# Six gather slots instead of eight, and one weight block kept in the freed room, in a two-layer decoder trunk

## What is computed

```
for l in range(DEPTH):                      # 2 layers
    x = x + mixer_l(rmsnorm(x))             # even: GLA + stick-breaking; odd: MoBA + RG-LRU
    x = x + memory_cross_attention(rmsnorm(x), rmsnorm(mem), ...)
    x = x + peer_ffn(rmsnorm(x), wq, subkeys, u, v)

def block(xi):                              # peer_ffn, for 128 tokens
    q = (xi @ wq).reshape(Tb, PEER_HEADS, 2, PEER_DQ // 2)
    s = jnp.einsum('thcd,hcnd->thcn', q, subkeys)
    ...                                     # top 16 of 128 x 128 key pairs for each of 8 heads
    ue = u[eidx]                            # eidx: 128 tokens x 8 heads x 16 experts
    ve = v[eidx]
    act = jax.nn.gelu(jnp.einsum('td,thkd->thk', xi, ue), approximate=False)
    return jnp.einsum('thk,thkd->td', (g * act), ve)
```

## Time and profile before

| | |
|---|---|
| median of 3 runs | 1721.77 us (1721.43 to 1725.01) |
| the profiled execution | 1724.17 us, its span 1722.4 us |
| PE busy | 1354.3 us, 79% of the span |
| DVE busy | 991.8 us, 58% |
| ACT busy | 717.6 us, 42% |
| POOL busy | 608.0 us, 35% |
| moved by DMA | 670.05 MB, 389 GB/s over the span |

### The profile page before, as it was taken

How to read it: one execution, slowest core, us unless ns; L and a number is a source line. 1 busy time by engine, 2 the same in 40 slices (tenths; PEclk the granted TensorE clock), 3 DMA queues, 4 the chain that set the end, 5 groups by cost and what they waited for, 6 DMA issues and landing times.

```text
span 1722.4 us, 24057 instructions
## 1 busy us (share of the span) xinstructions
PE 1354.3 (79%) x8582; PEld 702.3 (41%) x8582; DVE 991.8 (58%) x2464; ACT 717.6 (42%) x1990; POOL 608.0 (35%) x516
## 2 busy tenths in 40 slices
PE   8797999896798859787787669787788566766766
PEld 7676855553374216344354115344464111111111
DVE  1421498754567856654556876664548964445443
ACT  2322246544533434563533444563534443333332
POOL 0000122343333343233333453232334456655552
PEclk9898999898898979988889669998898676567566
DMA  9513799999999999999999999999999999999996
GB/s 385 202 49 123 303 424 421 379 407 422 422 421 423 420 423 423 421 422 422 421 421 422 421 407 424 421 421 422 422 421 404 422 421 421 421 421 421 421 421 255
DMA packets 86904, 670.05 MB, mean 389 GB/s; under 512 B 9584, under 2 KB 12032, under 8 KB 13568
## 3 DMA queue, kind: packets, MB, share of 16 engines
q0 software_dynamic: 73728, 536.90, 75.2%
q1 hardware_dynamic: 13056, 131.61, 18.6%
HBM read 667.43 MB, written 1.05 MB: 388 GB/s over the span
## 4 chain that ended last, share of the span: by engine, by line
DMA 41%; PE 38%; DVE 10%; ACT 5%; issue 4%; POOL 2%; SPq 0%; POOLq 0%; ACTq 0%; DVEq 0%; PEldq 0%
DMA arena<-in_experts,idxT 40%; PE psum L579 37%; DVE arena L1637 5%; POOL arena L2056 2%; ACT cst L1066 1%; ACT ring L1066 1%; DVE red L1606 1%; DVE cst L1598 1%; ACT gains L1066 1%; ACT L1066 1%; DMA ring<-in_ev_sq 0%; ACT gelus L1066 0%; DVE cst L1604 0%; PE psum L963 0%; ACT L1071 0%
## 5 line engine op out<-in xcount | busy, mean ns | idle before, releaser
L2056 POOL DMA_INDIRECT arena<-in_experts,idxT x512 | 607.8, 1187 | 1086.2 <-PE psum L579 831.2
L579 PE MATMUL psum<-arena,cst 64*64 64x512 f32 (+1 forms) x4102 | 687.7, 758 | 284.9 <-ACT cst L1066 283.8
L1637 DVE CUSTOM_DVE_ANT_0 arena<-arena,xrow 128x1024 f32<-128x1024 f32 x512 | 622.8, 1224 | 501.5 <-DMA arena<-in_experts,idxT 500.4
L1066 ACT ACTIVATE gelus<-red 128x1 f32<-128x1 f32 x512 | 103.4, 202 | 742.5 <-DVE red L1637 741.5
L579 PEld LDWEIGHTS psum<-arena,cst 64*64 64x64 f32 (+1 forms) x4102 | 130.3, 154 | 678.4 <-ACT cst L1066 599.5
L579 PEld LDWEIGHTS psum<-hT,ring 128*128 128x128 f32 x2368 | 285.0, 198 | 116.6 <-issue 110.7
L579 PE MATMUL psum<-hT,ring 128*128 128x128 f32 x2368 | 306.7, 287 | 25.1 <-DVE hT L1481 21.5
L1066 ACT ACTIVATE cst<-cst,gains 128x128 f32<-128x128 f32 x512 | 206.3, 403 | 16.8
L1066 ACT ACTIVATE gains<-gelus,gateT 128x1 f32<-128x1 f32 x512 | 150.8, 294 | 18.5 <-DVE gateT L1615 1.5
L579 PEld LDWEIGHTS psum<-mixT,ring 128*128 128x128 f32 (+1 forms) x592 | 70.1, 193 | 27.9 <-issue 25.4
L579 PE MATMUL psum<-mixT,ring 128*128 128x128 f32 (+1 forms) x592 | 76.9, 283 | 3.7 <-issue 3.0
(11 more groups left out here) (225 smaller groups left out, 844.9 us busy)
## 6 DMA issues: line engine op xcount, KB each, us to landing
ring<-in_pq SPq DMA_DIRECT2D x16, 2048.0 KB, 11.6
ring<-in_ev_out SPq DMA_DIRECT2D x4, 2048.0 KB, 9.6
ring<-in_xq SPq DMA_DIRECT2D x4, 2048.0 KB, 11.5
ring<-in_xo SPq DMA_DIRECT2D x4, 2048.0 KB, 11.5
arena<-in_experts,idxT POOLq DMA_INDIRECT x512, 15.3
ring<-in_od_out SPq DMA_DIRECT2D x4, 2048.0 KB, 12.0
ring<-in_ev_sq SPq DMA_DIRECT2D x2, 2048.0 KB, 10.2
ring<-in_ev_sk SPq DMA_DIRECT2D x2, 2048.0 KB, 12.2
```

The costliest lines, as they stand in the source:

```text
L579: return nc.tensor.matmul(out, lhsT, rhs, start=start, stop=stop)
L1066: return nc.scalar.activation(out, in_, f, **k)
L1637: V.tensor_tensor_reduce(out=ut, in0=ut, in1=xrow[:, u // PAIRS, :], scale=1.0, scalar=0.0, op0=ALU.mult, op1=ALU.add, accum_out=dots[:, k ...
L2056: nc.gpsimd.indirect_dma_start(slot[slot_of(u)], None, d["experts"], bass.IndirectOffsetOnAxis(ap=idxT[:, u:u + 1], axis=0))\
```

## The change

The slots of expert rows become six. The room of the other two (columns 12288 to 16383 of `arena`) becomes a fifth place for weights, number 4. `HELD` names one block for each layer that goes there: `ev_sq` and `od_rx`. Each is loaded once, for the front of the first half, and kept until the front of the second half has read it; `ev_sq1` and `od_rx1` vanish from the list. The other blocks alternate between the ring's slots as before, but counted without the held ones. Since 256 is no multiple of 6, the slot of a unit now counts through both layers.

```
+HELD = {"ev_sq": 4, "od_rx": 4}
...
-SLOTS = 8
+SLOTS = 6
...
     for t in range(TT):
         for n in ("sq", "sk", "sv", "qk", "gv", "gr"):
-            out.append((f"ev_{n}{t}", d[f"ev_{n}"], f"{n}.{t}"))
+            if t == 0 or f"ev_{n}" not in HELD:
+                out.append((f"ev_{n}{t}", d[f"ev_{n}"], f"{n}.{1 if f'ev_{n}' in HELD else t}"))
...
-    for b in range(len(blocks)):
-        s = b % RING if b < early else b % 2 if b < late else (b - late) % LATER_RING
+    turn = 0
+    for b, name in enumerate(names):
+        turn = 0 if b in (early, late) else turn
+        if name[:-1] in HELD:
+            s = HELD[name[:-1]]
+        else:
+            s = b % RING if b < early else turn % 2 if b < late else turn % LATER_RING
+            turn += 1
...
+        places = [ring[:, s, :] for s in range(RING)] + [arena[:, 3 * BLOCK:4 * BLOCK]]
...
-        def slot_of(u):
-            return (u + 1) % SLOTS
+        def slot_of(l, u):
+            return (l * UNITS + u) % SLOTS
...
-            eng.wait_ge(gathered[slot_of(u)], 16 * (l * UNITS // SLOTS + u // SLOTS + 1))
+            eng.wait_ge(gathered[slot_of(l, u)], 16 * ((l * UNITS + u) // SLOTS + 1))
...
                     if l or u >= SLOTS:
                         taken(pool, l, u - SLOTS)
```

More of the change, by code:

```diff
@@ L182, in weight_blocks @@
         for n in ("rx", "mq", "mk", "mv", "rg"):
-            out.append((f"od_{n}{t}", d[f"od_{n}"], f"{n}.{t}"))
+            if t == 0 or f"od_{n}" not in HELD:
+                out.append((f"od_{n}{t}", d[f"od_{n}"], f"{n}.{1 if f'od_{n}' in HELD else t}"))
         out += [(f"out1{t}{b}", d[f"od_out{b}"], f"out1{t}.{b}") for b in range(2)]
@@ L399, in trunk @@
         psum_free = [sem(f"psum_free{b}") for b in range(BANKS)]
-        w_loaded = [sem(f"w_loaded{b}") for b in range(RING)]
+        w_loaded = [sem(f"w_loaded{b}") for b in range(RING + 1)]
         in_x, in_small = sem("in_x"), sem("in_small")
@@ L523, in load @@
                     sp.wait_ge(k_norm, 4)
-                dst = ring[:, s, :].rearrange("p (k n) -> p k n", n=src.shape[2])
+                dst = places[s].rearrange("p (k n) -> p k n", n=src.shape[2])
                 sp.dma_start(dst, src).then_inc(w_loaded[s], 16)
@@ L573, in weights @@
             def weights(name, shape3=None):
-                s, n, _ = PLACE[AT[name]]
+                s, n, _ = PLACE[AT[name[:-1] + "0" if name[:-1] in HELD else name]]
                 pe.wait_ge(w_loaded[s], 16 * (n + 1))
-                return ring[:, s, :].rearrange("p (k n) -> p k n", n=shape3 or 512)
+                return places[s].rearrange("p (k n) -> p k n", n=shape3 or 512)
             def mm(out, lhsT, rhs, start=True, stop=True):
@@ L600, in experts @@
                     pe.wait_ge(weighed, l * UNITS + u + 1)
-                    v = slot[slot_of(u)][:, D:2 * D]
+                    v = slot[slot_of(l, u)][:, D:2 * D]
                     for b in range(2):
@@ L1634, in unit @@
                 landed(dve, l, u)
-                ut = slot[slot_of(u)][:, 0:D]
+                ut = slot[slot_of(l, u)][:, 0:D]
                 k = u % PAIRS
@@ L2055, in _ @@
                         taken(pool, l, u - SLOTS)
-                    nc.gpsimd.indirect_dma_start(slot[slot_of(u)], None, d["experts"],
+                    nc.gpsimd.indirect_dma_start(slot[slot_of(l, u)], None, d["experts"],
                                                  bass.IndirectOffsetOnAxis(ap=idxT[:, u:u + 1], axis=0))\
-                        .then_inc(gathered[slot_of(u)], 16)
+                        .then_inc(gathered[slot_of(l, u)], 16)
 def kernel(**inputs):
```

## The result

The changed kernel takes 1754.37 us (median of 4 runs, 1751.05 to 1763.66) against 1722.83 us (4 runs): a ratio of 1.0189, 95% interval 1.016 to 1.0219. The forecast was 1726.1, the range 1716.5 to 1736. The direction was right, the size was not. The profiled execution is the slowest of the four, 1763.66 us (span 1761.9), so its differences to the profile before add up to 39.5 us, not to 31.5.

The account below looks back on a forecast made before the run. DMA engines were taken to bound most of the kernel, PE some fronts. -4.5 for a missing load, +7.5 for six slots and +1.3 for earlier loads gave +4.3 us, 1726.1 us; range 1716.5 to 1736.

Parts of the forecast that it names:

- What bounds: Most of the kernel: DMA engines bound at about 421 GB/s, 2.49 us a unit, eight slots always full.
- The missing load in layer 1: Load at 1057.22 us disappears where DMA bounds: -4.5 us, with ends of -5 and -2.
- The missing load in layer 0: Load issued at 227.75 us disappears, but PE's work hides it before as after: 0, at best 2 us gain.
- Six slots: Gathers issued later make units 43, 256, 330 and 384 late, at 7.0 us to landing: +7.5 us in sum.
- The walk: Search through all units for issue of u + 2 plus 7.0 behind u's dot products on a waiting DVE: +7.5 us.
- The steady stretch: Where units come at 2.49 us, six slots leave 10 us for a gather, over the shortest landing of 6.4: no cost.
- The loads that come earlier: Before 550 us, od_rx0 follows xv1 at once and delays gathers; unit 113 lands later: +1.3 us.
- The three loads: Over units 128 to 159, od_mv0 joins od_mq0 and od_mk0; same bytes, DMA bounds them: 0.
- every front starves: In seven front stretches the queue of six runs dry once, 5.0 us each: about 1752 us, chance 0.13.

Follow-up runs that it names:

- two small loads: Kernel before, eight slots, but the second loads of ev_sq and od_rx bring one eighth of the block: 1716.59 us, ratio 0.9958.
- the loads as of old: Changed kernel, but od_rx0 and od_mv0 wait as in the kernel before, back at their old places: 1752.11 us, ratio 1.0157.
- the clash at unit 280: Kernel before with seven slots for units 104 to 279, half of od_rx held; units 279 and 280 share a slot: 1727.93 us, ratio 1.0002.

## Why the prediction was wrong

- **What bounds** the kernel was right: DMA at 421 GB/s, 2.49 us a unit, eight slots always full in the last stretch. The runs agree: seven eighths of two loads are worth 7.4 us, of 8.7 at most. The last stretch keeps its 2.49 us a unit with six slots.
- **The missing load in layer 1**, -4.5: the profiles show -4.1, -4.5 and -2.7. The chain there is a piece of PE now, as I had feared, and still half of the 5.0 us or more were there to have:

```profile
1062.62 10.96 DMA arena<-in_experts,idxT
...
1078.31 31.69 PE psum L589 x251
```

- **The missing load in layer 0**, 0: not confirmed. The profile of two small loads shows no gain there, but its median has 4.4 us more of gain than the profile. PE as a cover for the slots was wrong; six slots alone cost 2.7 us by unit 16 and 8.5 by unit 48 in the stretch that I had left out because PE was busy for 101.31 of 106 us. DMA was at 420 GB/s in the same row. Both were full at once, so taking DMA's queue away cut PE's piece in two.
- **Six slots**, +7.5: this is the step that failed. Six slots alone cost 32 us. What failed is the way of counting late units. I counted only units for which DVE stood waiting, and asked whether one gather would come in time for them. What is lost is time of the DMA engines, wherever too few gathers are under way, also where landed units still lie ready; in a kernel that DMA bounds later on it does not come back.

  The gathers are too few where a front holds a slot long after the landing: 5.1 us from a landing to the next issue in its slot in the last stretch, 7.5 us at the median before unit 384, 13.5 us for unit 15, all in the trace before.

  The walk was incomplete even by its own rule: it names one unit at each of four places, at the first of them unit 43 (2.0) and not unit 42 (3.0), and leaves out other places, as that of unit 111, where issue of unit 113 at 567.01 plus 7.0 lies 3.6 us behind the dot products at 570.37. By that rule the worst units of all places add up to some 15 us. With 7.0 us, but set against every unit's landing, they add up to 33 us; with the 8.1 us of three gathers in a round 47 us, for 117 gathers of 512 in 15 places. These are estimates from the trace before, made afterwards. With 33 in the place of 7.5 the sum is +30 us where 31.5 were measured; 47 is too much, as the worst units of neighbouring places can count one loss twice.

  The time to landing is the smaller part of the miss: the first gathers after the pause of the changed kernel landed in 5.5 to 6.5 us, so 7.0 was not low for one gather, but three in a round need 8.1 us and 0.8 to the next issue, and under 3.6 gathers on their way the rate falls. The steady stretch was right, by a narrow margin: 10.0 us or four gathers, where three already lose 14% of the rate.
- **The loads that come earlier**, +1.3: od_rx beside xv1 can be read from the table between units 48 and 112 only together with other things (the change loses 10.7 us there and 12.6 in its second profile, six slots alone 5.8, with the loads as of old 9.5, so 1.2 to 3.1 are left for it). The three loads, which I had put at 0, cost 6.5 - 2.8 = 3.7 us in one profile and nothing in the other. In the medians this is within the noise.
- **The rivals**: the third one, "every front starves" with 1752, was nearest, at 1754.4. I gave it 0.13. Its mechanism was the case, its sum in part luck: it had 5.0 us for each of seven stretches, and with six slots alone the table has 8.5 us by unit 48, 0.1 from unit 216 to 232 and 11.2 from 280 to 384. Its condition, more than 6 x 2.49 less 6.4 = 8.5 us from landing to the next issue in the slot, could have been looked up: it is met by 131 units in the trace before, all of them ahead of unit 384. What I held against it, that loads keep the queue long, is true as far as it goes. With six slots alone 3.4 gathers are under way in the mean when a load starts and 4.5 when it ends, and the rate holds meanwhile. It does not help in the stretches between the loads, and there the 33 us are lost.
- The Trainium skill's fit in "DMA: Bandwidth & Descriptors", section "Anatomy of one DMA — SWDGE (gpsimd) path", from which an estimate of 4.4 us for 1 MB follows, would have led further away still: no gather in any of these runs landed in under 5.2 us, and three in a round took 8.1.

What stays open: how much the moved loads cost in the median (0 to some 5 us), what layer 0's load is worth with eight slots, and what half a block is worth in a table of slots without the clash at unit 280.

## What to carry to other kernels

A pool of slots for a DMA stream has a share that is under way and a share that is in use. Measure by itself how many must be under way for the full rate, with a wait that limits only that: here four of 1 MB run at 420 GB/s and three at 360. Then look up the share in use where it is longest, and not in the mean: from a unit's landing to the next issue in its slot. Here the eighth slot was worth 5 us and the seventh 26, against 5.0 us at most for a block of weights, so the room must be priced by the queue and not only by the bytes it saves.

## What the runs showed of the hardware

With three indirect gathers of 1 MB under way the 16 DMA engines move 360 GB/s in the stretch without a front, and with four 420. The time to landing is 8.1 us with three, 9.2 with four and 15.0 with the eight slots of the kernel before. I had not expected an edge as sharp as that. The busy share of the DMA engines hardly shows it: it is 0.96 with three under way and 1.01 before, while the rate falls by 14%, since packets of 8 KB take 349 ns in the mean where they took 314. A gather issued when hardly any other was under way landed in 5.5 to 6.5 us (units 21 to 23 of the changed kernel). Executions of six slots alone and of the change spread over 10 and 13 us, with three under way over 19, with seven slots over 10, with four under way over 9, and those of the kernel before over 4 to 6.
